# Turning and masking the gated MLP's spatial weights ahead of the feature transposes of the token mixing

## The reference

```python
for l in range(DEPTH):                                   # DEPTH = 2
    x = x + FFN_RESID * swiglu_ffn(rms_norm(x, ffn1_norm[l]), ffn1_w_in[l], ffn1_w_out[l])
    h = rms_norm(x, mix_norm[l])
    uv, c_q, c_kv, k_rope, z, xbc, dt_raw, gates = jnp.split(h @ w_in[l], IN_OFFSETS, axis=-1)
    y_a = gmlp_mixer(uv, gm_v_norm[l], gm_w_s[l], gm_b_s[l])
    y_b = mla_mixer(...)                                 # attention over latents
    y_c = ssd_mixer(...)                                 # state-space scan
    ...                                                  # gates, w_branch, w_out
    x = x + FFN_RESID * swiglu_ffn(rms_norm(x, ffn2_norm[l]), ffn2_w_in[l], ffn2_w_out[l])

def gmlp_mixer(uv, v_gain, w_s, b_s):
    u, v = jnp.split(jax.nn.gelu(uv, approximate=False), 2, axis=-1)
    v = rms_norm(v, v_gain).reshape(bsz, s // GM_CHUNK, GM_CHUNK, GM_GROUPS, GM_GROUP_DIM)
    w = jnp.where(causal[None], w_s, 0.0).astype(v.dtype)            # causal: lower triangle
    sp = jnp.einsum('gts,bcsgd->bctgd', w, v) + b_s.T[:, :, None].astype(v.dtype)
    return u * sp.reshape(bsz, s, GM_WIDTH)
```

## Time and profile before

| | us |
|---|---|
| median of 3 runs | 2389.71 |
| lowest and highest run | 2387.39, 2391.09 |
| the profiled execution | 2389.52 |
| its span, first to last instruction | 2387.8 |
| TensorE busy | 2264.0 (95%) |
| VectorE busy | 1252.0 (52%) |
| ScalarE busy | 948.1 (40%) |
| GpSimd busy | 113.9 (5%) |

### The profile page before, as it was taken

How to read it: one execution, slowest core, us unless ns; L and a number is a source line. 1 busy time by engine, 2 the same in 40 slices (tenths; PEclk the granted TensorE clock), 3 DMA queues, 4 the chain that set the end, 5 groups by cost and what they waited for, 6 DMA issues and landing times.

```text
span 2387.8 us, 33269 instructions
## 1 busy us (share of the span) xinstructions
PE 2264.0 (95%) x12878; PEld 1734.5 (73%) x12878; DVE 1252.0 (52%) x2287; ACT 948.1 (40%) x1694; POOL 113.9 (5%) x96
## 2 busy tenths in 40 slices
PE   5999999998999899879999899999999999999999
PEld 3877784543577455368888689888788896798887
DVE  4724544111333411167754666777677636666776
ACT  2532212111322211054444654654555446645543
POOL 1000000000000000000014200000000052000000
PEclk9999999999999999989999999999999999999999
DMA  9976468999713899956654325466466535153663
GB/s 349 319 236 234 159 258 374 430 429 423 269 71 148 374 429 429 411 151 188 184 165 161 121 71 203 133 203 193 148 199 192 187 109 176 38 197 119 212 185 96
DMA packets 310253, 535.63 MB, mean 224 GB/s; under 512 B 14894, under 2 KB 200944, under 8 KB 296304
## 3 DMA queue, kind: packets, MB, share of 16 engines
q1 hardware_dynamic: 309180, 532.61, 61.9%
q10 hardware_dynamic: 948, 1.28, 0.2%
HBM read 532.81 MB, written 1.05 MB: 224 GB/s over the span
## 4 chain that ended last, share of the span: by engine, by line
PE 85%; DVE 7%; ACT 3%; issue 2%; DMA 2%; SPq 1%; POOL 0%; POOLq 0%; ACTq 0%; DVEq 0%
PE bank L601 15%; PE bank L1070 14%; PE bank L892 13%; PE yacc L930 9%; PE bank L897 7%; PE bank L585 5%; PE yacc L807 2%; PE yacc L618 2%; PE bank L636 2%; PE bank L1010 2%; PE bank L1285 1%; PE yacc L1082 1%; PE bank L672 1%; PE yacc L1229 1%; PE bank L766 1%
## 5 line engine op out<-in xcount | busy, mean ns | idle before, releaser
L1453 ACT ACTIVATE arena<-bank 128x256 f32<-128x256 f32 (+3 forms) x382 | 147.0, 407 | 575.4 <-PE bank L601 122.0
L892 PE MATMUL bank<-h_split,w_hi 128*128 128x512 f32 x1408 | 351.8, 392 | 0.0
L2362 DVE TENSOR_TENSOR w_lo<-wring,w_hi 128x1024 fp32r<-128x1024 f32 x264 | 307.4, 1218 | 3.3 <-ACT w_hi L1676 3.3
L1676 ACT ACTIVATE w_hi<-wring 128x1024 fp32r<-128x1024 f32 x264 | 277.7, 1056 | 49.4 <-PE yacc L930 49.2
L892 PEld LDWEIGHTS bank<-h_split,w_hi 128*128 128x128 f32 x1408 | 259.4, 189 | 50.1
L897 PEld LDWEIGHTS bank<-h_split,w_lo 128*128 128x128 f32 x1408 | 193.6, 191 | 20.5 <-issue 4.0
L897 PE MATMUL bank<-h_split,w_lo 128*128 128x256 f32 x1408 | 201.8, 285 | 3.8 <-ACT h_split L1587 3.6
L2972 POOL TENSOR_TENSOR wx_lo<-wring,wx_hi 128x1024 fp32r<-128x1024 f32 x42 | 107.4, 2559 | 1905.4 <-ACT wx_hi L1493 1905.4
L1070 PE MATMUL bank<-arena 128*64 128x512 f32 x672 | 169.9, 599 | 12.0 <-issue 8.6
L1070 PE MATMUL bank<-wring,arena 128*64 128x512 f32 x768 | 168.9, 593 | 10.6 <-issue 6.8
L1688 ACT ACTIVATE H<-bank 128x256 f32<-128x256 f32 x176 | 67.4, 383 | 253.1 <-PE bank L897 253.1
(11 more groups left out here) (409 smaller groups left out, 3799.2 us busy)
## 6 DMA issues: line engine op xcount, KB each, us to landing
wring<-in_ffn_w_in SPq DMA_DIRECT2D x176, 512.0 KB
wring<-in_w_ada SPq DMA_DIRECT2D x24, 2048.0 KB
wring<-in_ffn_w_out SPq DMA_DIRECT2D x88, 512.0 KB
wring<-in_w_in SPq DMA_DIRECT2D x20, 2048.0 KB
wring<-in_moe_w_down SPq DMA_DIRECT2D x16, 2048.0 KB, 23.4
wring<-in_moe_w_gate SPq DMA_DIRECT2D x16, 2048.0 KB, 18.9
wring<-in_moe_w_up SPq DMA_DIRECT2D x16, 2048.0 KB, 22.2
arena<-in_moe_w_gate SPq DMA_DIRECT2D x12, 2048.0 KB, 15.1
```

Source lines behind the costliest of these rows:

```text
L892: return mm(b[:, :], r(w_hi[:, j % 2, g, c * HB:(c + 1) * HB]), r(h_split[:, c, :, :].rearrange("p a t -> p (a t)")), start=start, stop=st ...
L1453: ins = f(dst, bank_of(name)[0:dst.shape[0], 0:T] if src is None else src, func, **kw)
L1676: f(w_hi[:, j % 2, part, :].bitcast(F32R), wring[:, u % WSLOTS, part * DC * HB:(part + 1) * DC * HB], ACT.Copy).then_inc(w_hi_ready[part], 1)
L2362: tt(w_lo[:, j % 2, part, :].bitcast(F32R), wring[:, (u0 + j) % WSLOTS, part * DC * HB:(part + 1) * DC * HB], w_hi[:, j % 2, part, :], ALU ...
```

## The change

In each layer the four transposes of the spatial weights, with their wait for the load and their bank, go on TensorE from behind the `kv` results to ahead of `turn_features(mxl)`. On VectorE the masked product goes from between queries and keys to ahead of `token_rstd()`, so behind the residual sum of the feed-forward half. No instruction is added or removed. The bank numbers of all results from `mxl.x0` to `kv1.1` move on by one; from `u` on they are as before.

```diff
--- before.py
+++ after.py
@@ -1271,9 +1271,14 @@
                 if l:
                     turn_features(f"f1{l}", 3 * l)
                 swiglu(f"f1{l}")
+                t = f"m{l}."
+                pe.wait_ge(spatial_landed, 2 * 16)
+                b = fill(f"{t}wT")
+                for g in range(GMG):
+                    last = nc.tensor.transpose(b[:, g * P:(g + 1) * P], gmw[:, l, g, :], ident[:, :])
+                filled(f"{t}wT", last)
                 turn_features(f"mx{l}", 3 * l + 1)
                 scale_rows()
-                t = f"m{l}."
 
                 def unit(tag, k, n):
                     return weights(t + tag)[:, 0:k * n].rearrange("p (k n) -> p k n", k=k)
@@ -1331,11 +1336,6 @@
                         token_major(f"{t}kv{i}.{g}", i, w[:, :, g * 512:(g + 1) * 512], ckv, 512)
                 used_by(f"{t}kv1.1")
 
-                pe.wait_ge(spatial_landed, 2 * 16)
-                b = fill(f"{t}wT")
-                for g in range(GMG):
-                    last = nc.tensor.transpose(b[:, g * P:(g + 1) * P], gmw[:, l, g, :], ident[:, :])
-                filled(f"{t}wT", last)
                 weights(f"{t}u", wait=False)
                 for m in range(4):
                     part_product(f"mix{l}", 13 + m, x_hi, x_lo)
@@ -2532,6 +2532,10 @@
             layer_norm("ln11", 1, 1, between=lambda: ffn_weights(0))
             for l in range(DEPTH):
                 half_step(2 * l)
+                t = f"m{l}."
+                dve.wait_ge(*full(f"{t}wT"))
+                moved(f"{t}wT", tt(wT, bank_of(f"{t}wT")[:, :].rearrange("p (g t) -> p g t", g=GMG),
+                                   rows(upper[:, 0, 0:P], GMG), ALU.mult))
                 token_rstd()
                 dve.wait_ge(rbc_ready.sem, rbc_ready.upto("dve"))
                 for k in range(DC):
@@ -2583,11 +2587,6 @@
                     dve.wait_ge(rope_ready.sem, rope_ready.upto("dve"))
                 for n, src in enumerate((Qt, Kt)):
                     ss = sm[:, 96 + 16 * n:112 + 16 * n]
-                    if n:
-
-                        dve.wait_ge(*full(f"{t}wT"))
-                        moved(f"{t}wT", tt(wT, bank_of(f"{t}wT")[:, :].rearrange("p (g t) -> p g t", g=GMG),
-                                           rows(upper[:, 0, 0:P], GMG), ALU.mult))
                     dve.wait_ge(qkss_ready.sem, qkss_ready.upto("dve"))
                     v.tensor_reduce(ss, qksq.rearrange("p (h d) -> p h d", d=QK), AX.X, ALU.add).then_inc(qkstd_ready.sem, 1)
                     dve.wait_ge(qkstd_ready.sem, qkstd_ready.upto("dve", 2))
```

## The result

The changed kernel takes 2393.32 us, the median of 22 runs (2386.21 to 2397.21). The kernel before, run beside it on the same chip, takes 2389.44 (22 runs, 2386.59 to 2392.87). The ratio is 1.0014, with a 95% interval of 1.0008 to 1.0020, so the change costs 1.9 to 4.8 us. That is under the 0.2% that the prediction treats as no change, but the sign is settled by this comparison, and it is the other one. The predicted 2388.8 us and its range up to 2391.0 miss it. Two further sets of runs of the changed kernel, each beside fresh runs of the kernel before, gave 1.0005 (0.9994 to 1.0016) and 1.0019 (1.0010 to 1.0028).

What follows compares the result with a forecast made beforehand. TensorE was taken as the bound (85% of the span). Transposes removed ahead of "u" give -0.45 - 0.46 = -0.91 us, added work is hidden, clock nothing: from 2389.71 to 2388.8 us, range 2386.3 to 2391.0.

Steps and rivals of the forecast that it cites:

- The move at "u": TensorE ahead of the "u" products: four transposes leave the path, u0 starts earlier, 0.45 us in layer 0, 0.46 in layer 1.
- The cover at the opening: Ahead of the row scale: added transposes (0.45 us) and masked product (0.68 us) hide in idle time before VectorE's reciprocal.
- A smaller step that failed: GpSimd's low half of u2's weights moves by the same 0.45 us as u0, with 0.05 us over.
- Given back: Rival: around "u" to "z", a follower that does not move with TensorE eats the 0.91 us; 2389.7 us, chance 0.14.
- the part on the clock: Opening's idle stretch: the clock's fall stays, so nothing is taken; bounds -2.0 to +0.5 us per layer.
- clock kept: Rival: at the opening, extra transposes put off the clock's fall until the products have begun; 2385.3 us, chance 0.06.
- its other 1.5 us: Opening, first layer: without the clock's fall the first 24 products end at 1246.05, not 1247.52.
- Clock falls ahead of "u": Rival: at the stop before "u" the clock falls and slows the products, 3.1 us per layer; 2395.0 us, chance 0.03.
- the sign by which the prediction wanted to be found wrong: Ahead of the "u" products: a granted clock under 1.00 would show the prediction wrong.

Runs made afterwards that it cites:

- the one with the opening alone: Kernel before, with only the first four of the sixteen turns of X made twice; 2392.36 us, ratio 1.0008 (1.0000 to 1.0017).

## Why the prediction was wrong

**The part that was right.** The move at "u" takes the transposes off the path. u0 follows the stop, which is named for ScalarE's evacuation, and `dt` to "u" shrinks by 0.55 us in layer 0, where 0.45 was forecast. In layer 1, 0.25 came of the 0.46 in the first pair of traces (21.95 to 21.70 us), 0.39 between the means of all. The cover at the opening holds: the reciprocal follows ScalarE's root as before. The masked product was free in both places: the row scale starts no later, and "v" and the turns of queries and keys take 13.73 and 4.16 us in every trace, to 0.01 us. In layer 0, L2605, 2.52 us in the earlier trace rows beside GpSimd's split, takes 0.42 here (its line is L2604 now), for VectorE's rotation of the queries now ends before the split starts:

```profile
1318.42 0.42 DVE L2604 TENSOR_TENSOR arena<-arena 128x256 f32<-128x256 f32 x1
...
1319.25 2.41 POOL L2971 TENSOR_TENSOR wx_lo<-wring,wx_hi 128x1024 fp32r<-128x1024 f32 x1 [23.40 <-ACT wx_hi L1493]
```

That is a by-product of the loss, not a gain: u0's products run at the half level there, and the split starts 5.87 us behind u0 and not 4.35.

**A smaller step that failed.** The prediction let GpSimd's split move by the same 0.45 us as u0, with 0.05 us over. It does start 4.35 us behind u0 as before, but wherever the transposes are gone from "u" and the clock holds, it takes longer: 2.51 to 2.53 us in nine layers of the traces and 2.90 to 2.92 in four, where it took 2.38 to 2.40. It now starts among the last of VectorE's eight L2601 products (L2602 before), as the prediction said. In the nine layers one of these products then lasts until the split ends, 2.49 us instead of 0.29 in layer 0 of the kernel with the transposes behind the row scale; in the four none does, and it is the split that takes longer. That second way the prediction did not have. The price at "u" is 0.1 us in the nine and 0.5 in the four. So the 0.55 us that the move gives is nearer 0.45 net in most layers, the forecast's number by luck, and nearly nothing in the others. *Given back* is not what made the loss, but one of its followers is there, in layer 1 of the profiled execution above.

**The step that failed.** It is the part on the clock. It said that no row shows what four more transposes do to the fall, took nothing for them because an idle stretch of 1.8 us remains, and looked for a price only in the opening itself, -2.0 to +0.5 us per layer. In the opening itself -0.51 us came, inside these bounds. For the layer both the value and the bounds were wrong: by the table the clock costs 4.2 us in layer 0 (-0.51 + 0.18 + 3.07 + 1.49). The idle stretch remains at 2.00 us, and the clock still holds through it and through the row scale. That is what *clock kept* describes, with a chance of 0.06. It gave 0.5 us for the row scale, and -0.51 us is what came; of its other 1.5 us nothing came, since the return stayed where it was, 14.6 us behind the last feed-forward product.

Then the half microsecond turned into a loss, by a way that no rival had. The products start earlier, the return does not move, and so the 32 narrow products start 10.8 us behind the return instead of 11.1. In them the clock falls: +0.59 us in the narrow products and +2.48 us in the `xbc` products behind them. This is theory O. Its first half (the clock holds, the products come sooner, the return stays) is in layer 0 of all six traces of kernels with more transposes at the opening and uncut `kr`. Its second half, the fall in `kr`, is in five of them; in the sixth, with the transposes in both places, `kr` started 10.87 us behind the return instead of 10.78 to 10.82, so that the edge is under 0.1 us away. That the fall hangs on the unbroken run of 32 narrow products is shown by the kernel after with cut products: it is gone in both traces, while the opening is the same. (The cut also moves the first of them 2.8 us nearer to the return.) That the distance from the return decides is read from nine traces in which it goes with the fall, and from their second layers, where the distance is 11.9 to 12.4 us and no fall comes; no kernel was made that shifts `kr` by a chosen delay and leaves the opening alone, so this link is argued and not shown.

**The rival with the right place.** *Clock falls ahead of "u"* had a chance of 0.03 and a price of 3.1 us per layer. The fall is there, at 1314.2, though behind the stop: ahead of it the clock is 1.00, so that the sign by which the prediction wanted to be found wrong did not even show. Its condition was sound: it stood against itself that the stop stays 1.32 us, and the stop did not stay. It grew to 2.92 us because the q and kv products lost their own half-level stretch, which the kernel before had hidden in time that it would have waited anyway. Why no fall comes behind `dt` when one came in `kr` stays open; it is so in all five traces with a fall in `kr`. The price was twice too high: 1.49 us in one layer, for a half-level stretch of 3.3 us and not of the attention's 7.2. The cause is not that the transposes are gone: the kernel with both has the same stop of 2.92 us, and the one with the opening alone 3.02.

**What is due to what.** In layer 0: -0.51 and -0.55 us for the two gains, +3.07 for the fall in and behind `kr`, +1.49 for the one at "u", +0.18 on the way from `cq` to `kr`, where the first products wait for a return that does not come sooner. The trace of before had what would have warned: the clock already falls right behind narrow products there, behind `dt` (1292.80 to 1296.00 at 0.50, with TensorE busy all the while), and `kr` is made of the same kind. I had looked at no window between 1241.10 and 1308.40. The measured loss is still inside 0.2%, to which the prediction gave 0.91.

## What to carry to other kernels

Before work is moved into an idle stretch of TensorE at a stage's opening, list every stretch at the half clock level in the whole stage, with what runs in it, and ask of each whether it is hidden; a hidden one can be traded for one on the path. A run of narrow products is a place where the clock can fall, though TensorE is busy by the record. Here, cutting it into pieces between wide products took the fall away, and is worth a try. A change worth under a microsecond can move the clock by several, so it is judged by many runs and by two traces or more, never by its own term alone.

## What the runs showed of the hardware

- In layer 0 the moment at which the clock comes back was nearly fixed against the feed-forward half, 14.46 to 14.72 us behind its last product's start in the nine traces with uncut `kr` products, whether the clock had fallen 4.3 or 7.9 us behind it. Of the 0.51 us by which the products started sooner, 0.33 was left at `kr`.
- Four more transposes, 0.43 us of work (1234.88 to 1235.31) ahead of sixteen others, kept the full level through 2.00 us of idle time and the row scale in layer 0. The same idle stretch in layer 1 had a row scale of 0.71 us before and after. The Trainium skill (TensorE: Matmul & The Clock Gate, Part 4: PE-mode transpose) says that the full clock does not engage for transpose-mode work, as it does not count as busy in the same way. Whether the kernel's transposes are of that mode the rows don't say. If they are, these traces don't agree in full: four more of them, of the weights or of X, were enough to move the fall from 4.4 to 7.8 us behind the last feed-forward product.
- The clock fell in 32 products of 32 columns, with TensorE at 100% by the record, and the level stayed at 0.50 through 24 products of 256 columns behind them.
- The places of the clock vary from execution to execution of one program. Of the two traces of the kernel after with cut products, one had a further half-level stretch of 3.4 us near the end of the attention in both layers, 1.5 us each, and in its second layer the opening's fall at 7.9 us instead of 5.8.
- A VectorE instruction and a GpSimd split could lengthen each other when they ran together, and either could pay: L2605 took 2.52 us beside the split instead of 0.42, and the split 2.92 us instead of 2.38 when it started among VectorE's last L2601 products (layer 1 of the profiled execution).
